# Two hybrid layers and a mixture-of-experts layer: the order of the work between a layer's input projections and its output projection

## The chip, the cores and the metric

The kernel runs on one NeuronCore of one Trainium2 chip. The metric is the device time of one execution in microseconds (us). Before the change it is 1178.21 us, the median of three executions (1178.15, 1178.21 and 1180.46).

The core has five engines with a program each: PE (TensorE, matrix products and transposes), DVE (VectorE), ACT (ScalarE), POOL (GpSimd) and SP, which here only starts DMAs. They go through their programs in order and wait for one another through semaphores. Products land in PSUM, which has eight banks of 128 partitions x 512 fp32 values; POOL does not touch them in this kernel.

## The reference, cut to what matters

256 tokens with 1024 channels go through two layers (`first_block`, DEPTH = 2) and then through one layer of another kind (`second_block`). The change touches only the mixer of the first two. A mixer projects its normed input, runs a gated delta rule on four heads of 128 channels and a dilated softmax attention on eight heads of 64, joins both and projects back:

```python
def _gated_delta_rule(q, k, v, g, beta):        # per head, in chunks of 64 tokens
    G = jnp.cumsum(g, axis=-1)
    gamma = jnp.exp(jnp.where(incl, G[..., :, None] - G[..., None, :], -jnp.inf))
    kb = k * beta[..., None]
    a_kk = jnp.where(strict, jnp.einsum('bhnid,bhnjd->bhnij', kb, k) * gamma, 0.0)
    tri = a_kk + jnp.eye(C, dtype=f32)
    rhs = jnp.concatenate([v * beta[..., None], kb * jnp.exp(G)[..., None]], axis=-1)
    sol = lax.linalg.triangular_solve(tri, rhs, left_side=True, lower=True, unit_diagonal=True)
    qk = jnp.einsum('bhnid,bhnjd->bhnij', q, k) * gamma
    ...
    def step(state, xs):                         # over the chunks
        v_new = u_c - jnp.einsum('bhcd,bhde->bhce', w_c, state)
        o_c = jnp.einsum('bhcd,bhde->bhce', qg_c, state) + jnp.einsum('bhij,bhje->bhie', qk_c, v_new)
        state = state * dc_c[..., None, None] + jnp.einsum('bhcd,bhce->bhde', kd_c, v_new)
        return state, o_c

def _dilated_attention(q, k, v):                 # (window, dilation) = (128,1), (512,4), (2048,16)
    ...                                          # softmax per dilation over the keys it reaches,
    wts = jax.nn.softmax(jnp.stack(lses), axis=0)  # merged by the softmax denominators
    o = jnp.einsum('gbsh,gbshd->bshd', wts, jnp.stack(outs))
```

The kernel works in chunks of 128 tokens, two for each head (NT = 2), so there are eight triangular matrices of 128x128 ("units", u = 2 x head + chunk). It takes the three dilations as one softmax with one mask table (`dilmask`).

## The kernel before, in words

A layer is 102 weight tiles of 128x1024 values. SP loads each into a ring of six slots; ACT copies it into a high part and DVE subtracts that to get the low part ("refill", L2165 and L2460), into one of three slots that PE reads. Tiles 0 to 27 of a layer are the mixer's input projections, 28 to 35 its output projection (T_WOUT = 28), and the rest belongs to the feed-forward block. After tile n, `refill(n)` readies tile n + 3.

The change is in what stands between tile 27 and tile 28. No weight tile is used there. On PE it is, in this order:

1. **The heads' start.** L1909 turns the rows of log decays and betas into columns (`cols`). For each head i, L1918 and L1920 broadcast the decay row and the beta row over the partitions into bank i % 2; three transposes (L1842, called with `qkvs` and `qkn`) bring two value tiles and a key tile to token order in bank 6 + i % 2; L1934 and L1935 form the keys' products with keys and with queries (the Gram matrices) in bank 2 + i % 2. ACT takes exp(G) and beta from the broadcast (L2296, L2297), DVE forms the differences of the decays (L2628), ACT exponentiates them (`gam`, L2303) and scales the value and key tiles (L2307, L2311), POOL multiplies beta and `gam` (L2831), and DVE multiplies both Gram matrices from PSUM (L2639 for `qkt`, L2641 for `bp`). Then DVE makes the first inverse block: `bp` times the mask of level 0 (L2646), and the identity minus that (L2649).
2. **The levels.** The triangular matrices are inverted by doubling of blocks. Levels 1 to 4 each take X = bl x tinv (L1997), a copy of X by ACT (L2355), Y = uinv x X (L2007), and `tinv` minus Y on DVE (L2683); eight transposes (L1842) and ACT copies (L2348) give `uinv` from `tinv`. `bl` is `bp` times the mask of the level, made by POOL (L2839), in two slots by the parity of the level. Levels 5 and 6 work on 32x32 and 64x64 blocks (L2021 to L2053).
3. **The recurrence** over the two chunks (L2059 to L2088).

The attention's eight heads are laid between these steps by a function `attend(i)` on PE, ACT and DVE. On PE, `attend(i)` holds the scores of head i (L1847, L1848), the transposes of the probabilities of head i - 2 (L1842 x3) and, for every second i, the products with the values of two heads (L1967 to L1971). On DVE it holds the mask and the two maxima of head i (L2659 to L2663) and then the norm of head i - 1 (L2668 to L2671); on ACT the exponentials of head i (L2318, L2320) and copies for head i - 2 (L2328). In a level, PE runs X, the transposes of the level before, `attend`, and then Y; DVE runs all of `attend` ahead of the two subtractions. The first scores wait until DVE has taken all four heads' Gram matrices (`gram_used`).

In the rows, "region" stands for any of the small tiles that share one region of the memory, "bank" for a PSUM bank, "sq" for a tile that is used again for `tinv` and for the copies of X, and "y" for one that holds `bl`. "h" holds rotated queries and keys.

## Time and profile before

| | |
|---|---|
| median of 3 executions | 1178.21 us |
| the profiled execution, its time | 1178.6 us |
| its span, first to last instruction | 1176.8 us |
| PE busy | 1137.5 us (97%) |
| DVE, ACT, POOL busy | 802.8, 702.0, 59.8 us |
| mean granted TensorE clock | 0.978 |

The span is 1.8 us shorter than the execution that it was taken from, and that execution 0.4 us longer than the median. The clock is a share of TensorE's full 2.4 GHz; 0.5 is its lower level, 1.2 GHz. A row of the timeline gives the start in us from the span's start, the duration in us, engine, line and operation with its operands, the count, and in brackets how long the engine stood idle before it and which instruction ended the idleness. Instructions of an engine are pipelined, so that the next row can start before the duration of the last is over: the distance of two starts is what an instruction costs its engine. A product of fp32 operands is two records. For PE "issue" means that nothing in the profile ended the idleness.

The steps that the change touches lie at 109 to 180 us in layer 0 and at 503 to 575 us in layer 1.

### The profile page before, as it was taken

The numbers are of one execution on the slowest core, as the hardware profiler recorded it, in microseconds if no ns is written. First come the engines' busy times: TensorE is split into PE (matmuls) and PEld (weight loads), VectorE is DVE, ScalarE is ACT, GpSimd is POOL, SyncE is SP. The second block draws the span as 40 slices with busy tenths as digits, with TensorE's granted clock in tenths as the row PEclk, the third lists the DMA queues.
The fourth block names the chain that finished last, engine by engine and source line by source line (L and its number), as shares of the span: only waits on it lengthen the run. The fifth ranks groups of instructions, "written<-read, shape, count | busy, mean of one in ns | idle before, by whom it ended". The sixth has DMA issues, their size and how long they took to land. (4 is left out here: it accounts for less than half of the span.)

```text
span 1176.8 us, 21324 instructions
## 1 busy us (share of the span) xinstructions
PE 1137.5 (97%) x7884; PEld 1034.5 (88%) x7884; DVE 802.8 (68%) x1312; ACT 702.0 (60%) x1233; POOL 59.8 (5%) x93
## 2 busy tenths in 40 slices
PE   8999899999999999989999999999999999999998
PEld 8999688899999899968889999998989887888886
DVE  5865545877777895564477777776875657558995
ACT  6664455755555776445566555566954446556784
POOL 0001500000000000150020000000000000000000
PEclk9999979999999999989899999999999989999999
DMA  7544103465656454411046656654432316667992
GB/s 255 180 156 132 37 1 90 153 197 179 190 175 190 140 178 147 146 55 37 19 127 205 193 182 182 177 193 121 150 118 81 106 45 242 233 185 279 357 348 82
DMA packets 50664, 184.26 MB, mean 157 GB/s; under 512 B 5664, under 2 KB 5824, under 8 KB 50464
## 3 DMA queue, kind: packets, MB, share of 16 engines
q1 hardware_dynamic: 49680, 180.12, 47.8%
q0 software_dynamic: 912, 3.16, 0.8%
q8 instruction: 47, 0.77, 0.3%
q14 instruction: 25, 0.20, 0.1%
HBM read 182.22 MB, written 1.05 MB: 156 GB/s over the span
## 5 line engine op out<-in xcount | busy, mean ns | idle before, releaser
L2460 DVE TENSOR_TENSOR w<-ring,w 128x1024 fp32r<-128x1024 f32 x240 | 292.6, 1221 | 127.6 <-ACT w L2165 127.5
L1754 PE MATMUL bank<-act,w 128*128 128x256 f32 x1216 | 347.5, 286 | 5.8 <-DVE act L2484 4.9
L1756 PE MATMUL bank<-act,w 128*128 128x256 f32 x1216 | 343.6, 283 | 0.0
L1755 PE MATMUL bank<-act,w 128*128 128x256 f32 x1216 | 343.5, 282 | 0.0
L2165 ACT ACTIVATE w<-ring 128x1024 fp32r<-128x1024 f32 x240 | 252.5, 1053 | 87.3 <-PE bank L1756 68.0
L1754 PEld LDWEIGHTS bank<-act,w 128*128 128x128 f32 x1216 | 232.6, 191 | 9.5 <-issue 7.2
L1755 PEld LDWEIGHTS bank<-act,w 128*128 128x128 f32 x1216 | 232.7, 191 | 2.1
L1756 PEld LDWEIGHTS bank<-act,w 128*128 128x128 f32 x1216 | 232.7, 191 | 0.0
L2757 DVE SCALAR_TENSOR_TENSOR region<-bank,pf,region 128x255 f32<-128x255 f32 (+1 forms) x176 | 84.8, 482 | 35.8 <-ACT region L2417 25.2
L1754 PE MATMUL bank<-w,hid 128*128 128x512 f32 x206 | 81.7, 397 | 0.0
L1755 PE MATMUL bank<-w,hid 128*128 128x512 f32 x206 | 81.5, 395 | 0.0
L1756 PE MATMUL bank<-w,hid 128*128 128x512 f32 x206 | 81.4, 395 | 0.0
L2417 ACT ACTIVATE region<-bank,pf 128x256 f32<-128x256 f32 x88 | 49.5, 563 | 47.3 <-PE bank L1756 42.2
L1754 PE MATMUL bank<-w,act 128*128 128x256 f32 (+1 forms) x208 | 73.2, 352 | 0.0
L1756 PE MATMUL bank<-w,act 128*128 128x256 f32 (+1 forms) x208 | 69.1, 332 | 0.0
L1755 PE MATMUL bank<-w,act 128*128 128x256 f32 (+1 forms) x208 | 69.1, 332 | 0.0
L2427 ACT ACTIVATE hid<-region 128x256 fp32r<-128x256 f32 x42 | 17.5, 417 | 66.8 <-DVE region L2739 66.8
L1756 PEld LDWEIGHTS bank<-w,hid 128*128 128x128 f32 x206 | 38.7, 188 | 9.5
L1754 PEld LDWEIGHTS bank<-w,hid 128*128 128x128 f32 x206 | 38.9, 189 | 7.5
L1755 PEld LDWEIGHTS bank<-w,hid 128*128 128x128 f32 x206 | 38.7, 188 | 7.4
L1754 PEld LDWEIGHTS bank<-w,act 128*128 128x128 f32 x208 | 39.4, 190 | 5.5 <-issue 1.0
L1756 PEld LDWEIGHTS bank<-w,act 128*128 128x128 f32 x208 | 39.4, 189 | 4.0
(446 smaller groups left out, 2053.6 us busy)
## 6 DMA issues: line engine op xcount, KB each, us to landing
ring<-wtiles SPq DMA_DIRECT2D x240, 512.0 KB, 3.6
ring<-etiles SPq DMA_DIRECT2D x33, 512.0 KB, 4.8
act_raw<-etiles SPq DMA_DIRECT2D x33, 512.0 KB, 5.1
sq<-etiles SPq DMA_DIRECT2D x22, 512.0 KB, 4.7
cst<-etiles SPq DMA_DIRECT2D x8, 512.0 KB, 5.2
region<-packp POOLq DMA_DIRECT2D x4, 512.0 KB, 4.5
cst<-consts SPq DMA_DIRECT2D x1, 1348.0 KB, 12.2
x<-xt SPq DMA_DIRECT2D x2, 512.0 KB, 5.9
```

The costliest lines, as they stand in the source:

```text
L1754: t.matmul(out_, still[:, 0], moving[:, 0], start=first, stop=False)
L1755: t.matmul(out_, still[:, 0], moving[:, 1], start=False, stop=False)
L1756: return t.matmul(out_, still[:, 1], moving[:, 0], start=False, stop=last)
L2165: a.activation(w_hi[:, s, :], ring[:, s, :], ACT.Copy).then_inc(hi_ready, 1)
L2417: a.activation(dst[:, q, :], bank[UP_BANKS[2 * q + w]][:, 0:S], ACT.Identity, scale=pf_("conv", p * 6 + w * 3 + 2), bias=pf_("bias", p * 2 ...
L2427: a.activation(last_hi if late else hid_hi[:, q, :], glu_p[:, q, :], ACT.Copy).then_inc(hi_done, 1)
L2460: v.tensor_tensor(w_lo[:, s, :], ring[:, s, :], w_hi[:, s, :].bitcast(F32), ALU.subtract).then_inc(lo_ready, 1)
L2757: ins = v.scalar_tensor_tensor(dst[:, q, j:], src[:, 0:S - j], pf_("conv", p * 6 + w * 3 + 2 - j), dst[:, q, j:], ALU.mult, ALU.add)
```

## The change

It does the following, in both layers:

- PE: the transposes of heads 0 and 1, then the broadcasts of all four heads, each in a bank of its own (0, 1, 5 and 4), then the Gram products of heads 0 and 1, then for heads 2 and 3 transposes and Gram products.
- ACT: all exponentials of the decays (`decay`) before the first value and key tile is scaled. It also copies the keys-queries product out of PSUM, which DVE multiplied from there before; a new semaphore `gram_free` tells PE that the bank is free.
- POOL: multiplies that copy with `gam` (four more instructions a layer). It no longer makes `bl` of level 1.
- DVE: all differences of the decays first; then for each head `bp`, the mask of level 0, the mask of level 1, and the subtraction from the identity.
- `attend` is cut in two on each engine: on PE `score` ahead of the transposes of `tinv`, and `values` behind Y; on DVE `masked` ahead of the subtractions and `normed` behind them.
- The refill of tile 30 (`T_WOUT - 1`) moves from behind tile 27 into level 2 on ACT and level 3 on DVE.

The diff, cut to its core:

```diff
+BC_BANKS = (0, 1, 5, 4)
...
@@ PE
+                def by_token(i):
                     if i >= 2:
                         pe.wait_ge(tr_act, l * 4 + i - 1)
...
+                def gram(i):
                     if i >= 2:
-                        pe.wait_ge(gram_used, l * 4 + i - 1)
+                        pe.wait_ge(gram_free, l * 4 + i - 1)
...
+                for i in range(2):
+                    by_token(i)
+                pe.wait_ge(proj_evac, l * 16 + 16)
+                for i in range(DNH):
...
+                    both = bank[BC_BANKS[i]]
+                    t.matmul(both[:, 0:S], ident[0:64, 32 + i:33 + i].to_broadcast([64, P]), rows[0:64, :],
+                             start=True, stop=True)
...
+                for i in range(2):
+                    gram(i)
+                for i in range(2, DNH):
+                    by_token(i)
+                    gram(i)
+                def score(i):
                     if i == 0:
                         pe.wait_ge(rope_done, l * 8 + 8)
-                        pe.wait_ge(gram_used, l * 4 + 4)
+                    if i < 2:
+                        pe.wait_ge(gram_free, l * 4 + 3 + i)
...
                 for lev in range(1, WIDE):
...
+                    score(lev)
                     if lev > 1:
                         transposed(lev - 1, tinv, lambda g: (t_ready, first_t + 2 * (lev - 1) + g + 1))
-                    attend(lev)
...
                         mm.then_inc(lev_y, 1)
+                    values(lev)
@@ ACT
+                for i in range(DNH):
+                    act.wait_ge(bc_done, l * 4 + i + 1)
+                    both = bank[BC_BANKS[i]]
+                    a.activation(eg1[:, i, :], both[:, P:S], ACT.Exp)
+                    a.activation(bbc[:, i, :], both[:, S:2 * S], ACT.Copy).then_inc(bc_act, 1)
+                    if i >= 1:
+                        decay(i - 1)
+                decay(DNH - 1)
...
+                    act.wait_ge(gram_used, l * 4 + i + 1)
+                    a.activation(qkt[:, 2 * i:2 * i + 2, :],
+                                 bank[2 + i % 2][:, :].rearrange("p (c w k) -> p c w k", c=NT, w=2)[:, :, 1, :],
+                                 ACT.Copy).then_inc(gram_free, 1)
...
+                    if lev == 2:
+                        refill(T_WOUT - 1)
@@ DVE
-                    v.tensor_tensor(qkt[:, 2 * i:2 * i + 2, :], pair[:, :, 1, :],
-                                    gam[:, i, :].rearrange("p (c k) -> p c k", c=NT), ALU.mult)
...
+                    masked = v.tensor_tensor(bl[:, 1, us], bp[:, us, :], level(1), ALU.mult)
...
                 for lev in range(1, WIDE):
-                    attend(lev)
+                    masked(lev)
                     for g in range(2):
...
                                         ALU.subtract).then_inc(t_ready, 1)
+                    normed(lev - 1)
+                    if lev == 3:
+                        refill(T_WOUT - 1)
@@ POOL
-                for lev in range(1, WIDE):
+                for lev in range(2, WIDE):
-                    if lev >= 3:
+                    if lev == 2:
+                        pool.wait_ge(u_ready, l * 2 * LEVELS + 2)
+                    else:
                         pool.wait_ge(lev_x, l * 2 * (LEVELS - 1) + 2 * (lev - 2))
...
+                        pool.wait_ge(gram_free, l * 4 + i + 1)
+                        pl.tensor_tensor(qkt[:, 2 * i:2 * i + 2, :].rearrange("p c k -> p (c k)"),
+                                         qkt[:, 2 * i:2 * i + 2, :].rearrange("p c k -> p (c k)"), gam[:, i, :], ALU.mult)
```

Line numbers of the changed kernel differ. On PE behind tile 27 of layer 0, this stands before the change (L1909 makes the columns, L1918 and L1920 are the broadcasts, L1842 the transposes, L1934 and L1935 the Gram products):

```order
L1909 MATMUL bank<-cst,region 128x64 x2
L1918 MATMUL bank<-region,cst 128x256
L1920 MATMUL bank<-region,cst 128x256
L1842 MATMUL bank<-cst,region 128x128 x3
L1934 MATMUL bank<-region 128x128
L1935 MATMUL bank<-region 128x128
L1934 MATMUL bank<-region 128x128
L1935 MATMUL bank<-region 128x128
L1918 MATMUL bank<-region,cst 128x256
L1920 MATMUL bank<-region,cst 128x256
```

and this after it (L1931 for L1909, L1844 for L1842, L1944 and L1946 for the broadcasts, L1923 and L1924 for the Gram products):

```order
L1931 MATMUL bank<-cst,region 128x64 x2
L1844 MATMUL bank<-cst,region 128x128 x6
L1944 MATMUL bank<-region,cst 128x256
L1946 MATMUL bank<-region,cst 128x256
L1944 MATMUL bank<-region,cst 128x256
L1946 MATMUL bank<-region,cst 128x256
L1944 MATMUL bank<-region,cst 128x256
L1946 MATMUL bank<-region,cst 128x256
L1944 MATMUL bank<-region,cst 128x256
L1946 MATMUL bank<-region,cst 128x256
L1923 MATMUL bank<-region 128x128
L1924 MATMUL bank<-region 128x128
```

All broadcasts now stand ahead of all Gram products, and the transposes of two heads ahead of the broadcasts.

On DVE in the same place, the first head before (L2628 the differences of the decays, L2639 `qkt`, L2641 `bp`, L2646 the mask of level 0, L2649 the subtraction):

```order
L2621 COPY region<-bank 128x128
L2628 SCALAR_TENSOR_TENSOR region<-bank,region,cst 128x128 x4
L2639 TENSOR_TENSOR region<-bank,region 128x256
L2641 TENSOR_TENSOR region<-bank,region 128x256
L2646 TENSOR_TENSOR region<-region,cst 128x256
L2649 TENSOR_TENSOR region<-cst,region 128x256
L2628 SCALAR_TENSOR_TENSOR region<-bank,region,cst 128x128 x2
```

and after (L2663 the differences, L2676 `bp`, L2679 the mask of level 0, L2680 that of level 1, L2682 the subtraction):

```order
L2657 COPY region<-bank 128x128
L2663 SCALAR_TENSOR_TENSOR region<-bank,region,cst 128x128 x8
L2676 TENSOR_TENSOR region<-bank,region 128x256
L2679 TENSOR_TENSOR region<-region,cst 128x256
L2680 TENSOR_TENSOR y<-region,cst 128x256
L2682 TENSOR_TENSOR region<-cst,region 128x256
L2676 TENSOR_TENSOR region<-bank,region 128x256
```

The four pairs of differences come first, and a head is still four instructions, one of them another one.

On PE in level 3, before (L1997 is X, L1842 x8 the transposes of `tinv`, L1847 and L1848 the scores, L1842 x3 the transposes of the probabilities, L2007 is Y):

```order
L1997 MATMUL bank<-sq,y 128x128 x8
L1842 MATMUL bank<-cst,sq 128x128 x8
L1847 MATMUL bank<-h 128x128
L1848 MATMUL bank<-h 128x256
L1842 MATMUL bank<-cst,region 128x128 x3
L2007 MATMUL bank<-sq,region 128x128 x8
```

and after (L2014 is X, L1849 and L1850 the scores, L1844 the transposes, L2024 is Y):

```order
L2014 MATMUL bank<-sq,y 128x128 x8
L1849 MATMUL bank<-h 128x128
L1850 MATMUL bank<-h 128x256
L1844 MATMUL bank<-cst,sq 128x128 x8
L2024 MATMUL bank<-sq,region 128x128 x8
L1844 MATMUL bank<-cst,region 128x128 x3
```

Nothing stands between the transposes of `tinv` and Y any more, and the transposes of the probabilities stand between Y and the next X.

## Rows read from the trace of the kernel before

**Rows 1.** Windows; columns: window, its length, busy us (instructions), PEclk, DMA share, GB/s.

```profile
109.07:126.54 17.47, 13.44 (x78) 10.33 (x77) 12.72 (x29) 8.80 (x28) 7.15 (x7) 0.93 0.16 61
126.54:132.98 6.44, 5.33 (x37) 4.72 (x37) 2.98 (x8) 3.65 (x11) 6.21 (x11) 0.92 0.00 0
132.98:152.64 19.66, 18.91 (x153) 16.68 (x153) 8.89 (x24) 11.11 (x29) 4.53 (x7) 1.00 0.16 55
152.64:173.42 20.78, 20.00 (x195) 16.63 (x193) 8.02 (x25) 10.39 (x30) 0.00 (x0) 0.67 0.00 1
502.96:520.93 17.97, 13.95 (x77) 10.73 (x77) 12.81 (x29) 8.80 (x28) 7.65 (x8) 0.88 0.23 60
520.93:527.98 7.05, 6.08 (x37) 5.46 (x37) 2.85 (x8) 3.65 (x11) 6.17 (x11) 0.82 0.00 1
```

**Rows 2.** Timeline of PE, layer 0, the heads' start; columns as told above.

```profile
109.89 0.69 PE L1918 MATMUL bank<-region,cst 64*128 64x256 f32 x2 [0.16 <-ACT region L2272]
110.95 0.55 PE L1842 MATMUL bank<-cst,region 128*128 128x128 f32 x3
111.33 0.39 PE L1934 MATMUL bank<-region 128*128 128x128 f32 x2
...
112.32 0.70 PE L1918 MATMUL bank<-region,cst 64*128 64x256 f32 x2
...
123.60 0.46 PE L1847 MATMUL bank<-h 64*128 64x128 f32 x2 [3.87 <-DVE region L2641]
```

**Rows 3.** Timeline of DVE, layer 0, the same stretch.

```profile
116.13 0.43 DVE L2646 TENSOR_TENSOR region<-region,cst 128x256 f32<-128x256 f32 x1
116.59 0.42 DVE L2649 TENSOR_TENSOR region<-cst,region 128x256 f32<-128x256 f32 x1
116.93 0.60 DVE L2628 SCALAR_TENSOR_TENSOR region<-bank,region,cst 128x128 f32<-128x128 f32 x2
...
121.59 1.20 DVE L2649 TENSOR_TENSOR region<-cst,region 128x256 f32<-128x256 f32 x1
...
125.07 0.54 DVE L2659 SCALAR_TENSOR_TENSOR region<-bank,cst 128x384 f32<-128x384 f32 x1
...
125.85 0.41 DVE L2663 TENSOR_REDUCE region<-region 128x1 f32<-128x256 f32 x1
```

**Rows 4.** Timeline of ACT, layer 0, one head's start.

```profile
113.48 0.28 ACT L2296 ACTIVATE region<-bank 128x128 f32<-128x128 f32 x1 [1.87 <-PE bank L1920]
...
113.92 0.42 ACT L2303 ACTIVATE region<-region 128x256 f32<-128x256 f32 x1
114.22 0.63 ACT L2307 ACTIVATE region<-bank,region 128x128 f32<-128x128 f32 x2
114.73 0.39 ACT L2311 ACTIVATE region<-bank,region 128x128 f32<-128x128 f32 x1
```

**Rows 5.** Timeline of PE, layer 0, level 2 and the start of level 3.

```profile
132.98 2.02 PE L1997 MATMUL bank<-sq,y 128*128 128x128 f32 x16 [1.11 <-DVE sq L2683]
134.84 1.04 PE L1842 MATMUL bank<-cst,sq 128*128 128x128 f32 x8
135.81 0.48 PE L1847 MATMUL bank<-h 64*128 64x128 f32 x2
...
136.66 0.55 PE L1842 MATMUL bank<-cst,region 128*128 128x128 f32 x3
137.04 1.95 PE L2007 MATMUL bank<-sq,region 128*128 128x128 f32 x16
139.37 2.02 PE L1997 MATMUL bank<-sq,y 128*128 128x128 f32 x16 [0.38 <-DVE sq L2683]
```

**Rows 6.** Timeline of ACT, layer 0, behind the transposes of level 4.

```profile
153.34 0.60 ACT L2348 ACTIVATE region<-bank 128x512 f32<-128x512 f32 x1 [0.66 <-PE bank L1842]
```

**Rows 7.** Timeline of POOL, layer 0.

```profile
121.23 1.28 POOL L2839 TENSOR_TENSOR y<-region,cst 128x512 f32<-128x512 f32 x1
...
135.89 2.01 POOL L2839 TENSOR_TENSOR y<-region,cst 128x1024 f32<-128x1024 f32 x1
```

More of the change, by code:

```diff
@@ L1937, in layer, with values @@
                     mm.then_inc(gram_done, 1)
[L1941 removed]
+                pe.wait_ge(rows_ready, l + 1)
+                pe.wait_ge(rope_used, l * 8 + 7)
+                for c in range(NT):
+                    mm = t.matmul(bank[4][:, S + 64 * c:S + 64 * c + 64], rows[0:64, c * P:(c + 1) * P],
+                                  ident[0:64, 0:64], start=True, stop=True)
+                mm.then_inc(cols_done, 1)
+                pe.wait_ge(qk_ready, l * 4 + 4)
+                for i in range(2):
+                    by_token(i)
+                pe.wait_ge(proj_evac, l * 16 + 16)
+                for i in range(DNH):
+                    if BC_BANKS[i] == 5:
+                        pe.wait_ge(rope_used, l * 8 + 8)
+                    if BC_BANKS[i] == 4:
+                        pe.wait_ge(cols_ready, l + 1)
+                    both = bank[BC_BANKS[i]]
+                    t.matmul(both[:, 0:S], ident[0:64, 32 + i:33 + i].to_broadcast([64, P]), rows[0:64, :],
+                             start=True, stop=True)
+                    t.matmul(both[:, S:2 * S], ident[0:64, i:i + 1].to_broadcast([64, P]), rows[0:64, :],
+                             start=True, stop=True).then_inc(bc_done, 1)
+                for i in range(2):
[4 more added lines that the diff above has]
+                def score(i):
                     if i == 0:
                         pe.wait_ge(rope_done, l * 8 + 8)
[L1944 to L1948 removed]
+                    if i < 2:
+                        pe.wait_ge(gram_free, l * 4 + 3 + i)
+                    else:
+                        pe.wait_ge(att_sm, l * 8 + i - 1)
+                    scores(i, raw[:, 0:4, :], raw[:, 4:8, :], bank[2 + i % 2]).then_inc(att_s, 1)
+                def values(i):
                     j = i - 2
@@ L2048, in layer @@
                     mm.then_inc(lev_x, 1)
+                values(LEVELS - 1)
                 for c in range(NT):
@@ L2693, in layer @@
                                     -1.0, None, ALU.mult).then_inc(u_ready, 1)
-                for i in range(LEVELS, SWAH + 1):
-                    attend(i)
+                masked(LEVELS)
+                for j in range(LEVELS - 1, SWAH):
+                    normed(j)
                 dve.wait_ge(rec_pe, l * 6 + 4)
```

174 lines of the change are left out of this document (75 added, 99 removed).

## The prediction

> **What bounds the kernel now.** I read the engines' busy time first: PE is busy 97% of the span, so what counts is where PE stands idle or runs at its lower clock. The list of waits then shows that between the input and the output projections PE's longest wait is the one for DVE before the first scores, 3.87 us [rows 2], and the windows, which I cut at the first instruction of each step (X of level 1 at 126.54, X of level 2 at 132.98, the transposes of level 4 at 152.64, the last products but two at 173.42), show the rest [rows 1]: 17.47 us for the heads' start with 13.44 us of PE work, 6.44 for level 1 with 5.33, 19.66 for levels 2 to 4 with 18.91, and 20.78 for the next stretch with 20.00. The first window's clock is 0.93 and the second's 0.92; layer 1 has 0.88 and 0.82 there and is 0.50 and 0.61 us slower in these two. The fourth stretch runs at 0.67: PE is idle only 0.78 us in it, but about two thirds of it are at half clock. DMA is at 0 to 0.23 of its time, so weights bound nothing here.
>
> So there are two prices: chains through DVE, ACT and back ahead of level 2, and the half clock of the last stretch. I work out the first by putting the new order together from the rows, with t = 0 at L1909 (109.07 in layer 0, 502.96 in layer 1).
>
> **The heads' start.** PE: the columns 0.7, six transposes at 0.38 per head (110.95 to 111.33 [rows 2]), so 1.45. A broadcast pair costs 1.06 (109.89 to 110.95 [rows 2]): the four end at 2.5, 3.6, 4.6 and 5.7. No broadcast waits for a bank any more, since each has its own. The Gram products of a head cost 1.0 (111.33 to 112.32 [rows 2]): those of heads 0 and 1 end at 6.7 and 7.7. ACT needs 0.44 behind each broadcast and 0.30 for each exponential (113.48, 113.92, 114.22 [rows 4]), DVE 0.6 for a pair of differences [rows 3]. The fourth pair thus ends at 5.7 + 0.45 + 0.65 = 6.8, and DVE begins `bp` of head 0 then. The refill of tile 30, which stood between, is gone from here; it now stands in levels 2 and 3, where ACT and DVE are busy 11.11 and 8.89 of 19.66 us [rows 1], so 1.1 and 1.2 us more fit, and nothing reads that tile before the output projection.
>
> A head on DVE stays at four instructions of 256 columns: 0.46 to an instruction that waits for the one ahead (116.13 to 116.59), 0.34 to one that doesn't (116.59 to 116.93 [rows 3]). The change sets the mask of level 1 between the two that wait for each other, so a head costs 0.46 + 3 x 0.34 = 1.5, and four cost 6.0: they end at 12.8. Before, each was 1.6 plus 0.6 for the differences.
>
> The last two subtractions before took 1.20 instead of 0.42 us, beside a mask on POOL (L2839 from 121.23 [rows 7], L2649 at 121.59 [rows 3]). POOL has no mask work now until all heads are through; only its last product with beta runs beside head 0, and I take 0.3 us for it, between 0 and two hits of 0.78. So the heads end at 13.1 (12.8 to 14.4). On this the Trainium skill, GPSIMD Engine Reference, section 1, says that the memory interface is shared and that DVE instructions with two SBUF inputs contend. The row agrees: 1.20 beside POOL, 0.42 alone. By the rule head 0's three such instructions could all be hit, which would be 2.3 us.
>
> Do the Gram products of heads 2 and 3 come in time? They now wait for ACT, which has the copy for `qkt` besides: ACT is through with the exponentials at 7.2, then per head 0.9 for scaling (114.22 to 115.12 [rows 4]) and 0.35 for the copy, a 256-column copy like L2297. Bank 2 is free at 8.5, bank 3 at 9.8; the products of head 3 end at 10.8, and DVE wants them at 11.3 (three heads after 6.8). That is 0.5 us of slack.
>
> The first scores (0.85) and the first four transposes of level 0 (0.49) fit in before 13.1. The last four (0.49) then release ACT, but X needs only the first group to begin: 13.1 + 0.55 = 13.65. Before it began at 17.47 and 17.97 [rows 1]. Gain **3.8 and 4.3 us**. PE now waits in four pieces, none over 0.7 us by this sum, where it waited 3.87 at once; so I take the clock at 1.0 here.
>
> **Level 1.** X costs 1.86 (132.98 to 134.84) and the scores 0.85 (135.81 to 136.66 [rows 5]), so Y begins 2.7 after X. DVE needs 1.2 for mask and maxima (125.07 to 126.26 [rows 3]) behind the scores and subtracts right away, 0.65, as the norm comes behind it: X of level 2 begins 2.7 + 0.1 + 1.2 + 0.65 + 0.05 = 4.7 after X of level 1. The exponentials of head 0 now stand ahead of the copies of X on ACT; they end some 2.1 after the heads are through, and the copies then are ready 0.6 ahead of Y. Before: 6.44 and 7.05 [rows 1]. Gain **1.75 and 2.35 us**.
>
> **Levels 2 to 4.** PE's work is the same. Removed is the wait of 0.38 for DVE ahead of X [rows 5]: the subtraction starts earlier, and the transposes of the probabilities (0.38) cover the rest. Added is a wait of Y for ACT. The first four transposes of `tinv` start at 152.64, ACT's copy starts at 153.34 and takes 0.60 [rows 6], so Y can begin 1.44 behind the first transpose; PE needs 0.97 (134.84 to 135.81 [rows 5]). Scores and more covered that before; now nothing does. The new wait is 0.47 a level. A level then costs 1.86 + 0.85 + 1.44 + 1.93 + 0.38 = 6.46 against 6.39 (132.98 to 139.37 [rows 5]): the two waits cancel. Level 4 has no wait ahead of its X of the next kind to give back, so the three levels **lose 0.6 us** (0.1 + 0.5). Its bounds are 0.3 gained, if the copy comes in time, and 1.4 lost. POOL's mask of level 4 takes 2.0 us [rows 7]; POOL now begins at 13.1 with 2.0, then four products of `qkt` (0.7 each) beside its old work, and ends the last mask near 28.8; X of level 4 comes at 31.
>
> **From the transposes of level 4 on.** The waits of 0.78 us [rows 1] can go, as Y and `values` now stand ahead of these transposes. In level 6 the exponentials of a head stand ahead of ACT's copies of `uinv` and PE has less to do meanwhile: I take 0.3 for this wait (0 to 0.8). Gain **0.5 us**, if the half clock stays as long as it was. It begins behind the products of 32x32 blocks, which stay.
>
> **The sum.** Layer 0: 3.8 + 1.75 - 0.6 + 0.5 = 5.4. Layer 1: 4.3 + 2.35 - 0.6 + 0.5 = 6.6. Together 12.0, from the profiled execution's 1178.6 to 1166.6; that execution is 0.4 above the median, so **1166.2 us**. Behind this stage PE goes on with work that the change leaves alone, so I let nothing take the gain back.
>
> **Rivals.**
> - A, the forecast: 1166.2, with 1163.5 to 1169 from the bounds above.
> - B, the half clock of the last stretch goes or shortens. 20.00 busy us at a mean of 0.67 mean 13.7 us at half, so at most 6.9 are to be had in a layer, and some 5 beside the chains. 1161 with one layer, 1156 with both. For it: the stretch becomes denser. Against: the small blocks that it follows stay, now with less full-width work between them. 0.13.
> - C, the start comes late: ACT has less slack than my 0.5 us, or POOL hits more of DVE's masks, or the half clock stays at level 1. By the bound of 14.4 and 1.1 us of clock (layer 1 against layer 0, 0.50 + 0.61) that is 2.4 a layer: 1171. 0.17.
> - D, slower: the half clock falls into the levels. The 0.47 us waits come in each level behind 64-row scores, and if the clock is given back there, 18.91 us of work [rows 1] double: +19 in one layer, 1185. It decides as soon as some 24 us more than now run at half, which would cost 12. Against: waits of 0.38 and 1.11 us stood there and the clock was 1.00 [rows 1]. The Trainium skill, TensorE: Matmul & The Clock Gate, on a second failure mode, says that frequent short idles between groups of products can make the clock swing. The rows of levels 2 to 4 do not show it with one short wait a level; by the rule this is the 1185. 0.04.
> - E, no change within 0.2% (some 2.4 us, about what a measurement of this kernel can tell from no change): C together with a longer half clock in one layer, or chains that I overlooked, 1177. 0.04.
>
> That leaves 0.62 for A. Faster: A + B + C = 0.92; same 0.04; slower 0.04. The range from 1160 to 1171.5 holds A, C and half of B.
>
> **What the changed profile would show.** Right: X of level 1 starts 13.3 to 14.4 us after the columns' products; no wait of PE over 1 us there and PEclk 1.00; X of level 2 about 4.7 later; in levels 2 to 4 PE waits for ACT's copies (the L2348 of now) about 0.5 before Y and not for DVE before X; the first two masks on DVE's heads at 0.42; PEclk 0.67 or so in the last stretch. Wrong: a wait of PE or DVE for the copy of `qkt`, instructions of 1.2 us among DVE's heads, a PEclk under 1.0 in the levels, or a last stretch at 1.00, which would be B.

## The result, and the profile after

The changed kernel takes 1164.9 us, the median of 20 executions (1163.35 to 1178.11), and the kernel before takes 1178.91 beside it (20 executions). The ratio is 0.990, with a 95% interval from 0.9873 to 0.9928: 1.0% faster, where 1166.2 us had been forecast. The profiled execution is the fastest of the 20, with 1163.35 us, a span of 1161.5 and a mean clock of 0.985; before it was 1178.6, 1176.8 and 0.978. So the two traces are 15.3 us apart, a little more than the medians.

The executions fall into two groups: 13 of 20 lie between 1163.4 and 1166.1 us (mean clock 0.982 to 0.985), and 7 between 1172.0 and 1178.1 (0.970 to 0.974). What makes the second group is found below.

The windows of the changed kernel, cut at the same instructions as before, with the columns of [rows 1]. The first four are layer 0, then come the first two of layer 1, and last the whole stretch between the end of one mixer's window and the start of the other:

```profile
108.91:122.20 13.29, 11.75 (x77) 9.85 (x77) 9.51 (x27) 9.33 (x31) 3.47 (x5) 1.00 0.12 40
122.20:127.04 4.84, 4.84 (x38) 4.23 (x37) 2.33 (x6) 3.14 (x10) 4.76 (x8) 1.00 0.00 0
127.04:146.88 19.84, 19.09 (x154) 16.68 (x153) 13.74 (x29) 11.56 (x29) 9.81 (x14) 1.00 0.23 81
146.88:166.12 19.24, 18.74 (x195) 15.33 (x193) 7.66 (x26) 11.27 (x32) 0.00 (x0) 0.73 0.00 1
495.67:508.97 13.30, 11.76 (x77) 9.86 (x77) 9.52 (x27) 9.32 (x31) 3.47 (x5) 1.00 0.15 41
508.97:513.81 4.84, 4.84 (x38) 4.22 (x37) 2.33 (x6) 3.15 (x10) 4.76 (x8) 1.00 0.00 0
166.12:495.67 329.55, 324.95 (x2369) 306.47 (x2367) 236.00 (x365) 199.43 (x333) 6.50 (x10) 1.00 0.51 161
```

Against [rows 1] the start is shorter by 4.18 us (4.67 in layer 1), level 1 by 1.60 (2.21), levels 2 to 4 are longer by 0.18 in each layer, and the last stretch is shorter by 1.54 (1.84, as it takes 19.29 in layer 1). That is 15.7 us. Between the two mixers nothing moved: the last window is 329.55 us now and was 329.54. The part ahead of the first start is 0.16 us shorter, and the rest of the program behind the second mixer's last window takes 608.6 us and took 608.0; so the spans differ by 15.3 us and not by 15.7. The start and level 1 have a clock of 1.00, where they had 0.82 to 0.93. The last stretch still runs at about 0.7.

The timeline of PE, layer 0 (start, us, line, times, wait and releaser), which answers to [rows 2] and [rows 5]:

```profile
110.30 0.70 PE L1944 MATMUL bank<-region,cst 64*128 64x256 f32 x2
110.83 0.59 PE L1946 MATMUL bank<-region,cst 64*128 64x256 f32 x2
111.26 0.59 PE L1944 MATMUL bank<-region,cst 64*128 64x256 f32 x2
...
116.52 0.55 PE L1844 MATMUL bank<-cst,region 128*128 128x128 f32 x3 [0.53 <-ACT region L2335]
...
119.62 0.46 PE L1849 MATMUL bank<-h 64*128 64x128 f32 x2 [0.40 <-ACT region L2338]
...
121.71 0.66 PE L1844 MATMUL bank<-cst,region 128*128 128x128 f32 x4 [0.61 <-DVE region L2682]
...
133.41 1.95 PE L2014 MATMUL bank<-sq,y 128*128 128x128 f32 x16
135.28 0.49 PE L1849 MATMUL bank<-h 64*128 64x128 f32 x2
135.61 0.59 PE L1850 MATMUL bank<-h 64*128 64x256 f32 x2
136.13 1.09 PE L1844 MATMUL bank<-cst,sq 128*128 128x128 f32 x8
137.48 2.05 PE L2024 MATMUL bank<-sq,region 128*128 128x128 f32 x16 [0.25 <-ACT region L2378]
```

The one wait of 3.87 us is now three of 0.40 to 0.61. A pair of broadcasts takes 0.96 us from its start to the next (110.30 to 111.26). In a level PE does X, scores, transposes and then waits 0.25 us for ACT's copy (L2378), and X waits for nothing.

The timeline of DVE in the same layer answers to [rows 3]: `bp` (L2676), mask of level 0 (L2679), mask of level 1 (L2680), subtraction (L2682), later the subtraction that ends level 1 (L2715) and a norm (L2703):

```profile
115.16 0.41 DVE L2676 TENSOR_TENSOR region<-bank,region 128x256 f32<-128x256 f32 x1
115.61 0.45 DVE L2679 TENSOR_TENSOR region<-region,cst 128x256 f32<-128x256 f32 x1
115.99 0.94 DVE L2680 TENSOR_TENSOR y<-region,cst 128x256 f32<-128x256 f32 x1
116.85 0.41 DVE L2682 TENSOR_TENSOR region<-cst,region 128x256 f32<-128x256 f32 x1
...
121.24 0.42 DVE L2682 TENSOR_TENSOR region<-cst,region 128x256 f32<-128x256 f32 x1
...
126.22 0.68 DVE L2715 TENSOR_TENSOR sq<-sq,bank 128x512 f32<-128x512 f32 x1
127.88 2.00 DVE L2703 TENSOR_SCALAR region<-region 128x128 f32<-128x128 f32 x1
```

And the timeline of POOL, with its product of beta and decays (L2869) and a mask (L2877), which answers to [rows 7]:

```profile
113.33 3.32 POOL L2869 TENSOR_TENSOR region<-region 128x256 f32<-128x256 f32 x4 [9.30 <-ACT region L2318]
121.73 2.00 POOL L2877 TENSOR_TENSOR y<-region,cst 128x1024 f32<-128x1024 f32 x1 [5.09 <-DVE region L2682]
127.79 2.00 POOL L2877 TENSOR_TENSOR y<-region,cst 128x1024 f32<-128x1024 f32 x1
```

Of DVE's sixteen instructions for the four heads one is long, the mask at 115.99 with 0.94 us, while POOL's last product runs until 116.65. No subtraction takes 1.20 any more.

### The profile page after: what moved, and what is told of

The parts are those of the page before. It is cut to its first block and busy times, and to the rows that moved or that the text cites. A ratio compares the mean times of both kernels' runs of the same rounds, so it can differ in the third digit from the quotient of the medians.

```text
span 1161.5 us, 21320 instructions
## 1 busy us (share of the span) xinstructions
PE 1128.9 (97%) x7884; PEld 1028.0 (89%) x7884; DVE 804.4 (69%) x1312; ACT 705.2 (61%) x1241; POOL 60.2 (5%) x97
```

## The experiments

Two questions were open. Which part of the change gives how much? And what sets the half clock of the last stretch, which came out 10.2 us long where it had been 13.7? (The lengths of such pieces are read from the clock's own record in the trace, which the PEclk of a window averages.) My theory for the second was that it follows how densely PE works in this stage: the denser, the less half clock. Where an experiment adds or takes away lines, its line numbers differ from the changed kernel's by a few.

**The changed kernel again.** No edit.

> The changed kernel once more. Of its 20 executions 13 took 1163.4 to 1166.1 us (mean clock 0.982 to 0.985) and 7 took 1172.0 to 1178.1 (0.970 to 0.974). Theory (clock): the second group has more time at half clock between the input and the output projections, since everything else of the program agrees to 0.4 us between the two kernels' traces; an execution of it should show a PEclk below 0.91 in that stage of one or both layers and 5 to 7 us more in each. Rival (elsewhere): the stage takes 57.2 us in each layer in the slow group too and the time is lost in the feed-forward or expert part. Expected: two thirds of the runs at 1163 to 1166, the others at 1172 to 1178.

Measured: six executions, 1163.51, 1165.81, 1166.03, 1166.31, 1174.79 and 1177.54 us; the profiled one is the slowest. The steps are 13.3, 4.84, 19.84 in both layers as in the first trace. The windows of `again`: the last stretch of both layers, then 30 us of the third layer:

```profile
146.48:166.75 20.27, 20.22 (x194) 16.38 (x192) 7.67 (x26) 11.25 (x32) 0.00 (x0) 0.66 0.00 1
534.29:554.91 20.62, 20.12 (x194) 16.71 (x192) 7.67 (x26) 11.26 (x32) 0.00 (x0) 0.67 0.00 1
870.00:880.00 10.00, 9.68 (x61) 9.49 (x59) 2.29 (x5) 1.45 (x4) 0.00 (x0) 0.71 0.16 54
880.00:890.00 10.00, 10.00 (x45) 9.35 (x45) 3.82 (x10) 1.94 (x6) 0.00 (x0) 0.50 0.14 52
890.00:900.00 10.00, 10.00 (x52) 9.33 (x52) 4.70 (x8) 2.59 (x7) 0.00 (x0) 0.60 0.17 54
```

The first of these three windows in the first trace of the changed kernel:

```profile
870.00:880.00 10.00, 10.00 (x86) 9.65 (x85) 3.98 (x11) 2.31 (x6) 0.00 (x0) 1.00 0.27 91
```

So the groups are not made in the stage. Here 23.9 us of the third layer run at half clock, in code that the change does not touch and while PE is hardly ever idle, and this costs about 12 us (half of 23.9). Of the thirteen traces with a changed kernel's code, four have such a piece there: `again`, and below `pool_mask`, `swap_3` and `swap_warm_2` (27.3 us each). They took 1177.54, 1180.8, 1170.94 and 1167.89 us; the three of them whose kernel has other executions lie among its slowest. The other nine have none there. The piece starts where small products do. This is the first row of 32 products with 4 columns each (64 records), which stand between wider ones:

```profile
871.19 0.58 PE L661 MATMUL bank<-cst,region 128*128 128x4 f32 x4 [0.32 <-ACT region L1026]
```

In `again` the half clock begins 3.0 us behind this row, at 874.1, and in the other three traces 2.1 to 2.9 us behind theirs. But the same products with the same wait of 0.32 us stand in the nine traces without the piece, so they do not bring it by themselves. What decides is open.

Within the stage the last stretch takes 20.27 and 20.62 us with 13.7 us at half clock, and in the first trace 19.24 and 19.29 with 10.2. So the length of that piece differs between executions of one program, and other traces show that it can differ between the two layers of one execution.

**The levels as before.** In each level PE has its transposes ahead of the scores again, and DVE the norm ahead of the subtractions:

```diff
@@ PE, levels
-                    score(lev)
                     if lev > 1:
                         transposed(lev - 1, tinv, ...)
+                    score(lev)
+                    values(lev)
                     for g in range(2):
                         ...                              # Y
-                    values(lev)
@@ DVE, levels
+                    normed(lev - 1)
                     ...                                  # tinv minus Y
-                    normed(lev - 1)
```

> The changed kernel with the order of levels 1 to 4 on PE and DVE as it was before (transposes, scores and probabilities ahead of Y; the norm ahead of the subtractions). Theory: the new order there is worth little: level 1 gets back about 0.9 us of wait for DVE (the norm of 0.8 us ahead of the subtraction), levels 2 and 3 take 6.39 again instead of 6.29, level 4 6.9 instead of 7.2 but with 0.24 of wait behind it. Sum: 1 to 1.5 us slower per layer than the changed kernel, so 1166 to 1167. Rival (the levels carry the gain): the subtraction ahead of the norm is what lets PE run on, and this kernel falls back by over 4 us, to 1169 or more.

Measured: 1168.57 us, the median of 11, against 1166.17 for `again`. Level 1 takes 5.98 us in place of 4.84, levels 2 to 4 take 19.89. The waits of PE (sum, times, longest):

```profile
PE bank L2014 <- DVE sq L2716: 2.1, 3, 1.1
```

The wait ahead of the X of level 2, 1.11 us in [rows 5], is back with 1.15, and the X of levels 3 and 4 wait 0.58 and 0.38. In level 1 the norm's place is all that differs, so there the early subtraction is worth 1.14 us a layer. In levels 2 to 4 this kernel changes two things at once, the norm's place on DVE and the order on PE, and they cancel: 19.89 us against 19.84. The kernel `swap`, below, takes them apart: with the early subtraction, the scores behind the transposes as here, and the values behind Y, these levels take 18.43 us.

**The start as before.** The new levels behind the old start. The diff shows PE's part; ACT, DVE and POOL have their old start too, with POOL's mask of level 1 and the refill of tile 30 in their old places:

```diff
-                for i in range(2):
-                    by_token(i)                          # keys' and values' transposes
...
-                for i in range(2):
-                    gram(i)
...
+                for i in range(DNH):
+                    if i >= 2:
+                        pe.wait_ge(bc_act, l * 4 + i - 1)
+                        pe.wait_ge(bc_dve, l * 4 + i - 1)
+                    ...                                  # broadcasts into bank i % 2, transposes, Gram
```

> The kernel before, with only the attention's split in two parts (scores ahead of the transposes, values behind Y, subtractions ahead of the norm) and the old start of the heads, old POOL masks and old place of the refill. Theory: the start is worth 4.2 to 4.7 us a layer plus up to 1 us of clock, and this kernel lacks it: 8 to 11 us over the changed kernel, so 1173 to 1175, with the wait of 3.87 us for DVE and a PEclk of about 0.9 ahead of level 2. Rival (the levels carry the gain): 1167 or less.

Measured: 1174.19 us, the median of 12. The waits of PE and the windows of the start and of level 1:

```profile
PE bank L1849 <- DVE region L2656: 3.9, 1, 3.9
```

```profile
108.28:126.21 17.93, 13.90 (x78) 10.70 (x77) 12.82 (x29) 8.79 (x28) 7.61 (x8) 0.91 0.19 59
126.21:132.72 6.51, 6.51 (x37) 5.86 (x37) 1.76 (x4) 3.37 (x10) 5.32 (x9) 0.73 0.00 0
```

The wait is back with 3.9 us, and with it a half clock of 6.8 us in both layers, which falls into the end of the start and into level 1 (0.91 and 0.73). Level 1 has no wait in it and still takes 6.51 us in place of 4.84 (5.73 in layer 1, where more of the piece falls into the start): all of that is the clock. The start is worth about 8 us of the medians, the larger part of the gain, and this includes what level 1 gets through the clock.

**The scores behind the transposes, the values where they are.** It takes the new wait for ACT away and keeps the rest:

```diff
-                    score(lev)
                     if lev > 1:
                         transposed(lev - 1, tinv, ...)
+                    score(lev)
                     for g in range(2):
                         ...                              # Y
                     values(lev)
```

> The changed kernel, with the transposes of tinv ahead of the scores again in levels 2 to 4, the probabilities still behind Y. Theory: Y's wait of 0.25 us for the copy of uinv goes (the scores, 0.85, cover it), and the subtraction of DVE, which comes behind mask and maxima of the scores, ends 0.9 us later after X but still inside the 0.38 of the probabilities or 0.1 beyond: 0.1 to 0.25 us less a level, 0.6 to 1.5 us less in all, 1162 to 1163. Rival: mask and maxima now hold the subtraction back and X waits for DVE by as much as Y waited for ACT: no change, 1163.5.

Measured: 1156.18 us, the median of 6, ratio 0.9807 (0.9754 to 0.986). The windows of levels 2 to 4 and of the last stretch, and a Y in PE's timeline:

```profile
126.43:144.86 18.43, 18.43 (x154) 16.59 (x154) 13.68 (x29) 11.46 (x29) 9.80 (x14) 1.00 0.26 88
144.86:164.07 19.21, 18.72 (x195) 15.31 (x193) 7.67 (x26) 11.25 (x32) 0.00 (x0) 0.73 0.00 1
```

```profile
135.93 2.05 PE L2024 MATMUL bank<-sq,region 128*128 128x128 f32 x16
```

The wait is gone and the levels take 1.41 us less in each layer, 5.82 for a level (X at 132.32 and 138.14) in place of 6.28. Of the 0.46 us the wait is 0.25; X and the transposes are 0.20 shorter. The last stretch of this trace is no faster than with the looser levels. But this trace does not stand for all: the median is 6 us under the 1162 to 1163 that I had expected. The other executions include 1153.34, 1153.95 and 1154.44 us, 10 us under the lowest of the 26 executions of the changed kernel, where the levels account for 2.8. Their mean clock is 0.990. In no trace with two pieces of 10.2 us or more is it above 0.985, so they had less half clock than that.

**The same twice more.** No edit to it.

> The kernel with the transposes ahead of the scores a second time (its six executions took 1153.3 to 1170.4 us). Its profile showed the three levels 1.41 us shorter in each layer, 2.8 in all, but its lowest time is 10 us under that of the changed kernel and its mean clock reaches 0.990 there. Theory: the other 7 us are half clock that fails to come, in the last stretch of the layers' mixer or in the later part of the program (942 to 984 us); a profile at 1153 should show 15 us less at half clock than the 39 of the first. Rival: they are in the levels themselves. Expected: the steps ahead of the half clock the same to 0.1 us, and 1153 to 1161.

> The swap kernel a third time, beside the next. So far ten executions: 1153.3, 1154.0, 1154.4, 1156.4, 1157.9, 1161.0, 1161.5, 1170.4, 1170.8, 1173.4. Theory: each is 1152 or so plus the half clock that it drew, 5 us for each layer's last stretch and some 12 where the third layer has a long one. Expected: the same spread, median 1154 to 1162, always under 1174.

Measured: 1166.14 us (4 executions) and 1167.14 (6). All 16 executions of this kernel lie between 1153.34 and 1173.42, with a median of 1161.8, and six have a mean clock of 0.986 to 0.990, where none of the 26 of the changed kernel is above 0.985. The last stretches of `swap_2`:

```profile
145.87:160.85 14.98, 14.17 (x195) 11.66 (x193) 7.66 (x26) 11.24 (x32) 0.00 (x0) 1.00 0.00 1
526.98:547.39 20.41, 20.19 (x194) 16.51 (x192) 7.66 (x26) 11.25 (x32) 0.00 (x0) 0.67 0.00 1
```

One program, one execution, two layers with the same work: 14.98 us without half clock and 20.41 with 13.7. So the half clock is worth 5.4 us here, and with the same order and the same density it comes or stays away. How often it comes in full does seem to depend on the order: 6 of 16 executions have a mean clock above 0.985, against 0 of 26 of the changed kernel. My theory had it so, but that density is the reason is not shown by that. `swap_3` has 19.22 us in both layers, and in the third layer 27.3 us at half clock.

**Work moved past the start of the last stretch.** The values of level 4 go behind the 32x32 products:

```diff
-                    values(lev)
+                    if lev < WIDE - 1:
+                        values(lev)
...
                 ...                                      # the 32x32 products
+                values(WIDE - 1)
```

> The swap kernel, with the probabilities' transposes and value products that stood behind Y of level 4 (1.2 us of full-width work) moved behind the first products of 32x32 blocks, on PE and ACT. Theory (density): the half clock of the last stretch follows the run of small-block work, 32x32 products, 64-row scores, 32x32 products; full-width work in the middle of it makes the stretch go without half clock more often, which is worth 5 us a layer (the step from the transposes of level 4 to the third-last products took 14.98 us without it and 19.2 to 20.6 with it). The move itself costs 0.2 to 0.5 us a layer, a wait of the transposes for DVE's subtraction. Expected then: 1150 to 1154. Rival (the clock does not care for this): the half clock stays at 10 to 14 us in both layers, and the time is that of swap, 1154 to 1161, or 0.5 worse.

Measured: 1158.32 us, the median of 6 (0.9741 to 0.9852). Windows of levels 2 to 4 and of the last stretch:

```profile
127.36:144.64 17.28, 17.28 (x140) 15.68 (x139) 12.67 (x25) 11.10 (x28) 9.79 (x14) 1.00 0.27 92
144.64:165.44 20.80, 20.23 (x208) 16.24 (x208) 8.65 (x28) 11.73 (x34) 0.00 (x0) 0.75 0.01 2
```

Together 38.08 us against 37.64 in `swap`: 1.15 us less in the one window and 1.59 more in the other, as the moved products now run partly at half clock. That piece stays 10.2 us long in both layers of this trace. So 1.2 us of such work (three transposes of 128x128 and six products on half of the array's columns) right behind the 32x32 products does not rule it out. The profiled execution is one of the slower ones; three of the six have a mean clock of 0.990 to 0.992 and 1153.38 to 1155.54 us, so whether the move makes the piece rarer stays open.

**Full-width work added.** Two times three products of 128x128 values, whose results nothing reads, in the midst of the small blocks:

```diff
+                for _ in range(3):
+                    t.matmul(bank[1][:, 0:P], ident, ones, start=True, stop=True)
                 ...                                      # 32x32 blocks, score(LEVELS - 1)
+                for _ in range(3):
+                    t.matmul(bank[1][:, 0:P], ident, ones, start=True, stop=True)
```

> The swap kernel with three products of 128x128 added behind the wait ahead of Y's 32x32 blocks, and three behind the scores ahead of the 64x64 blocks; their result is not used. Each costs 0.23 us at full clock, so 1.4 us a layer, of which 0.45 lie in a wait that is there anyway. Theory (density): more full-width work keeps the clock up in the last stretch, -5 us a layer in more executions, so 1148 to 1153. Rival (the clock does not care): 1.0 us a layer more, 1155 to 1163.

> The kernel with the six added products a layer a second time. Theory (density): its profile again has no half clock in the last stretch of either layer (step of 16.2 us from the transposes of level 4 to the third-last products), whereas of ten such stretches in the changed kernel and its variants so far nine had 10 to 14 us. Rival (chance): one or both layers show 10 to 14 us at half clock, a step of 20 to 22 us. Expected under the theory: 1152 to 1156, and 1164 to 1166 where the third layer has its long stretch.

Measured: 1160.53 and 1159.64 us (0.9773 to 0.9897, and 0.9759 to 0.9866), 6 executions each. The last stretches of `swap_warm`:

```profile
145.53:161.75 16.22, 15.86 (x207) 13.15 (x205) 7.66 (x26) 11.26 (x32) 0.00 (x0) 1.00 0.00 1
527.88:544.09 16.21, 15.85 (x206) 13.15 (x204) 7.65 (x26) 11.25 (x32) 0.00 (x0) 1.00 0.00 1
```

and that of layer 0 in `swap_warm_2` (layer 1 has 16.22 us at 1.00 too), with a piece of its third layer:

```profile
145.94:162.15 16.21, 15.85 (x206) 13.15 (x204) 7.66 (x26) 11.25 (x32) 0.00 (x0) 1.00 0.00 1
...
872.00:882.00 10.00, 10.00 (x49) 10.00 (x49) 2.13 (x8) 0.49 (x1) 0.00 (x0) 0.50 0.16 54
```

Four of four stretches are free of half clock. In the ten traces that have the changed start and no added products, 1 of 20 is, the one of `swap_2`. (The expectation of `swap_warm_2` speaks of one in ten; it was one in eighteen by then.) The traces alone overstate the contrast, as the clocks of `swap` and `swap_spread` show, but the executions without a trace bear it out: of the 12 with added products six have a mean clock of 0.992 to 0.994, and six have 0.982, as `swap_warm_2` has with its piece in the third layer and none in the stretch.

The added products do two things. They put wide work among the small blocks, and the second lot fills the only wait that stood ahead of the 64x64 blocks. The first row is the changed kernel's, the second `swap_warm`'s, behind which PE goes on without a wait:

```profile
152.66 1.31 PE L2065 MATMUL bank<-sq,region 64*64 64x64 f32 x16 [0.45 <-ACT region L2402]
151.64 0.94 PE L2061 MATMUL bank<-cst 128*128 128x128 f32 x6
```

No run takes the two apart, but the wait is not the cause by itself: layer 0 of `swap_2` has it, with 0.45 us, and no half clock, and in layer 0 of `again` the half clock begins at 150.5, ahead of that place and 7 us behind the last wait (0.25 us). The moved work of `swap_spread` was as long and did not keep the piece away; it stood in one place and filled half of the columns for most of its time, and which of these counts was not tried.

The added work costs 1.24 us a layer, 16.22 against 14.98, and saves some 3 us against a stretch with 10 us of half clock. The medians of all executions hardly differ, 1160.1 us of 12 against 1161.8 of 16 in `swap`, because the third layer's piece moves both by some 12 us. Parted by their mean clock into those that seem to have that piece and those that do not, they differ by 5.3 us (1165.6 against 1170.9) and 3.3 us (1153.9 against 1157.2). This parting was made after the fact.

**Mask of level 1 back on POOL.**

```diff
-                    masked = v.tensor_tensor(bl[:, 1, us], bp[:, us, :], level(1), ALU.mult)
...
+                for h in range(2):                       # on POOL
+                    pool.wait_ge(gram_used, ...)
+                    pl.tensor_tensor(bl[:, 1, us], bp[:, us], ..., ALU.mult).then_inc(bl_ready, 1)
```

> The changed kernel with the mask of level 1 made by POOL again, in two instructions behind heads 1 and 3. Theory: DVE's heads take 1.2 us instead of 1.5 each, but POOL's mask of heads 2 and 3 (1.3 us) starts only when head 3's product is there and X of level 1 waits for it; it also hits the last subtractions (1.20 instead of 0.42 us). X of level 1 starts 13.3 to 14.5 us after the columns instead of 13.29, so the whole is 0 to 2.5 us slower. Rival (the mask's place decides the start): X of level 1 falls back by over 2 us, towards the 17.5 of before.

Measured: one execution, 1180.8 us, of which 13 are the third layer's half clock (27.3 us). So it is read by its steps. The timeline of DVE and that of POOL:

```profile
117.60 1.20 DVE L2681 TENSOR_TENSOR region<-cst,region 128x256 f32<-128x256 f32 x1
120.88 1.20 DVE L2681 TENSOR_TENSOR region<-cst,region 128x256 f32<-128x256 f32 x1
```

```profile
117.19 1.33 POOL L2872 TENSOR_TENSOR y<-region,cst 128x512 f32<-128x512 f32 x1 [0.69 <-DVE region L2676]
120.47 1.33 POOL L2872 TENSOR_TENSOR y<-region,cst 128x512 f32<-128x512 f32 x1 [1.95 <-DVE region L2676]
```

Two subtractions take 1.20 us beside POOL's masks, and the start takes 13.94 us in place of 13.29 (13.88 in layer 1). So the start is 0.6 us shorter with the mask on DVE, although DVE does more there. In layer 0 level 1 takes 6.33 us with 3.4 at half clock, in layer 1 it takes 4.84. The waits of PE ahead of it are the same in both layers (0.5, 0.7 and 1.0 us), so they do not decide it.

**Gram products ahead of the transposes,** and all broadcasts ahead of both:

```diff
-                for i in range(2):
-                    by_token(i)
...                                                      # broadcasts, gram(0), gram(1)
-                for i in range(2, DNH):
+                for i in range(2):
                     by_token(i)
+                for i in range(2, DNH):
                     gram(i)
+                    by_token(i)
```

> The changed kernel with the keys' products ahead of the value tiles' transposes: broadcasts, Gram products of heads 0 and 1, transposes of heads 0 and 1, then for heads 2 and 3 the Gram product ahead of the transposes. Theory: the first broadcast starts 0.8 us earlier and so do the decays, and DVE's heads, which are the chain to X of level 1, start 0.8 earlier; ACT's scaling and the copy for qkt follow in the same order, the Gram products of head 2 no longer stand behind transposes that wait for ACT. X of level 1 at 12.4 to 12.9 instead of 13.29. Rival: ACT's scaling waits for the transposes that now stand behind, the bank of the Gram products comes free later, and X of level 1 is at 13.3 or later.

Measured: 1162.96 us, with steps of 13.29 and 4.85. The waits of PE:

```profile
PE bank L1923 <- ACT region L2338: 1.0, 1, 1.0
```

What the broadcasts gain, which start 0.9 instead of 1.4 us behind the columns, is lost in a wait of 1.0 us for a Gram bank. The start does not change, as the rival said.

**The refill of tile 30 back in the start.**

```diff
-                    if n < T_WOUT - 1:
-                        refill(n)
+                    refill(n)
```

> The changed kernel with the refill of tile 30 behind tile 27 again on ACT and DVE. Theory: ACT and DVE have room there, since DVE waits for the first broadcast until 3.2 us after the columns; ACT's refill ends at about 1.9 and DVE's at 3.1: X of level 1 within 0.2 of 13.29, and the levels unchanged, so no change. Rival: DVE's copy of the columns stands behind the refill, holds the first differences and the fourth broadcast back by 1.2 us, and X of level 1 comes at 14 or later.

Measured: 1166.67 us, steps of 13.3 and 4.84 in both layers. The refill's 1.23 us on DVE stand ahead of the heads' chain, which does not wait for them to end:

```profile
111.28 1.23 DVE L2492 TENSOR_TENSOR w<-ring,w 128x1024 fp32r<-128x1024 f32 x1 [1.81 <-ACT w L2186]
```

It had 1.81 us of idle time ahead of it. So moving the refill out of the start brings nothing.

## Why the prediction was right, step by step

**The start: 3.8 and 4.3 forecast, 4.18 and 4.67 measured.** The chain ran as it was put together, and the waits came in pieces under 0.7 us (three, not four) with the clock at 1.00, as stated. One thing came that had been named as a sign of being wrong: PE waits 0.40 us for the copy for `qkt` (L2338) ahead of the first scores. It cost nothing, as X of level 1 waited for DVE's last subtraction anyway (0.61 us ahead of the last transposes). Three sizes were off. A pair of broadcasts is 0.96 at a start and 0.86 later (0.43 each from 110.83 to 111.26), not 1.06; so `bp` of head 0 begins 6.25 us after the columns and not 6.8. The four heads then take 6.5 and not 6.3 (6.0 and 0.3 for POOL), as the mask beside POOL cost 0.94 - 0.42 = 0.52 more. They end at 12.75 in place of 13.1. On this the Trainium skill (GPSIMD Engine Reference, section 1) had said that DVE instructions with two SBUF inputs contend with POOL. The traces agree in kind: the mask of level 1 with two such inputs, which started while POOL's last product ran, was hit (0.94), and the `bp` with one input in PSUM was not (0.41), although it ran beside the product before. Of head 0's three instructions that could be hit, one was: the mask of level 0 began 0.2 us ahead of POOL's last product and took 0.45, and the subtraction came behind it. In `pool_mask` three of DVE's instructions were (0.83, 1.20 and 1.20).

**Level 1: 4.7 us forecast, 4.84 measured.** The gains are 1.60 and 2.21 against 1.75 and 2.35. The experiments divide them: 1.14 us is DVE's subtraction ahead of the norm (`old_levels`), the rest is the clock, and that came through the start (`old_start`).

**Levels 2 to 4: 0.6 us lost forecast, 0.18 measured.** The wait for ACT's copy came where it was said and was mis-sized twice: 0.25 us and not 0.47. Y begins 1.34 us behind the first transpose (129.85 to 131.19) and not 1.44; the rows had given 1.30 to the end of the copy (152.64 to 153.94), and no row showed the other 0.14. And the wait counts from the end of the transposes, 1.09 us behind their start, where I had taken the distance to the start of the next products, 0.97. `swap` shows the price of this order on PE: 1.41 us a layer.

**The last stretch: 0.5 us in each layer forecast, 1.54 and 1.84 in the first trace.** With the half clock at 13.7 us, as it was before, `again` has 20.27 and 20.62 against 20.78 and 21.13, which is 0.51 in both. That it is so exact is luck. The waits did go (PE is idle 0.05 and 0.50 us there and was 0.78 and 0.80), but other traces with 13.7 us at half clock and these orders take 20.28 to 20.63 us, which fits a piece that falls on other work each time. The rest, 1.03 and 1.33 us, is less half clock (10.2 in place of 13.7 us), the beginning of rival B. This too is the luck of the profiled execution, since `again` has 13.7 in both layers. Whether rival B's reason, a denser stretch, holds is open: the first two traces of one program differ without it, and `swap` with its denser levels goes without a full piece more often.

**The sum.** With the half clock as before the terms give 4.18 + 4.67 + 1.60 + 2.21 - 0.18 - 0.18 + 0.51 + 0.51 = 13.3 us, from 1178.6 to 1165.3, and the forecast was 12.0. Rivals C and E did not come, and neither did D: the clock is 1.00 in levels 2 to 4, although a short wait stands in each. The Trainium skill (TensorE: Matmul & The Clock Gate, on a second failure mode) says that frequent short idles between groups of products can make the clock swing; one wait of 0.25 us in each 6.3 does not do it in these levels in any of the traces.

What the prediction did not have is the second group of executions. It left "the work behind the stage" alone, and this holds for the work but not for its clock: 7 of 20 executions are about 11 us longer than the others (9 of 26 with `again`). The median lies in the lower group; had eleven of the 20 been long ones, it would have been past 1171.5, the end of the stated range. Nothing in the prediction said how many would be. The kernel before has such executions too, 11 of the 71 that were measured beside all these kernels, from 1187.2 to 1194.9 us, with mean clocks of 0.963 to 0.969 where they are on record. None of them was traced, so it is not shown that they have the same piece, nor whether the change makes it more frequent.

## What to carry to other kernels

Cut the time at the instructions that start each step and put the new order together from rows of its own kind: here this gave each term to within some 0.4 us, but for the half clock of the last stretch. When products end up right ahead of the instruction that needs their copy, that copy's whole way becomes a wait; let other work of PE stand between (the scores here, 1.41 us a layer). Before a difference of a few us is explained, look at the clock over the whole program in more than one trace: here a stretch that the edit does not touch moved an execution by 12 us, and one layer of a trace differed from the other by 5.4.

## What the hardware showed that was not expected

- PE runs at half clock while it is busy. In the last stretch of `again` it is busy 20.22 of 20.27 us at a clock of 0.66, and in its third layer 10.00 of 10.00 us at 0.50. In both places much of the work is small: 32x32 and 64x64 blocks, or products with 4 columns.
- The half clock of the last stretch was none, 10.2 or 13.7 us in these traces, and which it was changed from execution to execution and from layer to layer of one program. The idle wait of 3.9 us before the first scores went with 3.4 or 6.8 us each time (`before`, `old_start`). Behind waits of up to 1.15 us in the start and the levels (`old_levels`, `keys_first`) there was none, but for one layer of `pool_mask`.
- Six added products of 128x128 values took 1.24 us and kept the clock at 1.00 in four of four stretches; without them 19 of 20 traced stretches behind the changed start had 10.2 or 13.7 us of half clock. The mean clocks of the other executions say that with the order of `swap` it is rarer than these traces show, and that with the added products it stays away in all 12.
- POOL beside DVE can cost a multiple of the instruction's own time: a norm of 128x128 values, 0.31 us in the mean of 16 before, took 2.00 us beside POOL's mask (DVE at 127.88, POOL at 127.79), and a subtraction 1.20 in place of 0.42.
